# Query, key and value products of the latent vectors as three split products through the common weight ring

## The chip, the cores and the metric

The kernel runs on one core of a Trainium2 chip. The metric is the device time in microseconds (us). Of three runs before the change the median is 1682.95 us (1682.1 to 1685.35).

## The reference

An encoder of two layers works on 256 tokens of 1024 channels in float32. Each layer has three parallel branches (latent attention, a spatial gate, attention to a memory), merged by gates, and then a channel mixer: a dense SwiGLU in layer 0, eight experts with the best two per token in layer 1. The change touches the latent attention's projections:

```python
def mla_branch(c_q_raw, c_kv_raw, k_r_raw, positions, g_q, g_kv, w_uq, w_uk, w_uv):
    c_q = rmsnorm(c_q_raw, g_q)                     # 256 x 384
    q = (c_q @ w_uq).reshape(b, s, MLA_HEADS, MLA_QK)   # 384 x 768
    ...
    c_kv = rmsnorm(c_kv_raw, g_kv)                  # 256 x 256
    k_nope = (c_kv @ w_uk).reshape(b, s, MLA_HEADS, MLA_NOPE)   # 256 x 512
    v = (c_kv @ w_uv).reshape(b, s, MLA_HEADS, MLA_V)           # 256 x 512
```

## The kernel before

**Split products.** Nearly all weights reach TensorE (PE) in two parts of type fp32r: ScalarE (ACT) copies a piece from its raw float32 slot into the high part `whi` (`hi_parts`, line 1352), and VectorE (DVE) takes raw minus high into the low part `wlo` (`lo_parts`, line 1723). The activations are split in the same manner: ACT writes the high part out of PSUM with the norm's gain (`norm_hi`, line 1378), DVE the low part (`norm_lo`, line 1745). `acc3` (line 650) then makes three products per pair of tiles: high by high, high by low, low by high. The native float32 products go through `acc` (line 640) instead, which needs no split: the query, key and value projections do, and a few small ones.

**The ring.** `pieces` is one list in the order of use. SyncE (SP) loads piece after piece into raw slots; in the mixer three slots take turns (`MIX_RAW`), and slots 3 to 6 are scratch of the attention, except that the pieces `("uq", l, 0)` and `("ukv", l)` come early into slots 5 and 6. Before a load SP waits until the piece that was in the slot is used up (`wait_slot`): for a split piece that is its low part being written, for an unsplit one its last product. `("uq", l, 1)` stands unsplit in the common ring after the `qx` pieces. The split parts `whi` and `wlo` have three buffers each (`SPLIT`), so that split number m may begin when PE is done with piece m - 3.

**Who splits when.** ACT and DVE run a fixed order of instructions. Between their other work they call `hi_parts(room(name))` and `lo_parts(room(name))`. `room(name)` (line 582) counts the pieces whose earlier buffers PE has released before it makes the product `name`; all of these are split there, ahead of what follows in the program. For an unsplit predecessor in the same raw slot it also asks for that one's last product.

**The stretch of the change.** In each layer PE makes, in this order: the products of the input projection (`cq`, `ckv`, `sv`, `su`, `qx`), the transposes of the spatial weights (`wsT`, line 764), the transposes of the latent vectors (`cT`, line 681), the eight products of the spatial gate (line 778), which wait for ACT's copy of `wsT` (line 1445), the query products (lines 784 to 789), and then `mixer_steps`: memory scores of head 0 (`ms`, line 862), keys and values (`k`, `v`, lines 865 to 870), and "fill" steps of 18 split products of gate and branch weights (line 796) between the small products of the attentions. ACT has in this stretch the copy of `wsT`, the copies of the query products to `q_sb` (line 1451), the exponentials of the memory scores (line 1477) and the copies of the keys. DVE copies `qx` (line 1835), writes the latent vectors with their gain into `cT` (line 1842), mixes the spatial gate (lines 1853 to 1862), takes the maxima of the scores (line 1920), scales the probabilities (line 1928) and writes the values (line 1934). DVE's steps skip `lo_parts` at `ms` and `k` (line 1914), so that its first place for it after the query products is at step `v`. PE reads the latent vectors only when all three groups of `cT` are written (line 782).

Of the kernel before, what the change touches and what calls it, by code (L numbers as in the profile page):

```python
# [33 lines left out]
F32 = mybir.dt.float32  # L34
# [186 lines left out]
def build(nc, x, mem, positions, g_mix, w_in, g_q, g_kv, w_uq, w_uk, w_uv, g_sg, w_s, b_s, g_mem,  # L221
# [26 lines left out]
    with ExitStack() as ctx:  # L248
# [3 lines left out]
        def sem(name):  # L252
            return ctx.enter_context(nc.semaphore(name))
# [130 lines left out]
        gate_row_in = [sem(f"gate_row_in{i}") for i in range(4)]  # L384
        merged_hi = sem("merged_hi")
        pos_in = sem("pos_in")
        router_in = sem("router_in")
# [47 lines left out]
        def rows(w, c0, c1, r0=0, r1=None):  # L435

            r1 = w.shape[0] if r1 is None else r1
            return w[r0:r1, c0:c1].rearrange("(k p) c -> p k c", p=P)
# [14 lines left out]
        for l in range(DEPTH):  # L453
            wi, hk = w_in[l], D // 2

            def mixer_piece(key, *parts, **how):
                piece(key, MIX_RAW, *parts, **how)
# [7 lines left out]
            half_q = H * QK // 2  # L465
            mixer_piece(("uq", l, 0), rows(w_uq[l], 0, half_q), split=False, slot=RAW - 2)
            mixer_piece(("ukv", l), rows(w_uk[l], 0, H * NOPE), rows(w_uv[l], 0, BW), split=False, slot=RAW - 1)
            for name, c0, c1 in (("cq", 0, C_KV), ("ckv", C_KV, C_SG), ("sv", C_SG + SG, C_XQ)):
                for k in range(2):
                    mixer_piece((name, l, k), rows(wi, c0, c1, k * hk, (k + 1) * hk))  # L470
            for name, c0 in (("su", C_SG), ("qx", C_XQ)):
                for n in range(2):
                    mixer_piece((name, l, n), rows(wi, c0 + n * W, c0 + (n + 1) * W))
            mixer_piece(("uq", l, 1), rows(w_uq[l], half_q, 2 * half_q), split=False)
            for n in (1, 2, 0):
# [89 lines left out]
        def free(ins, name):  # L565
            ins.then_inc(bank_free[groups[name].bank], 1)

        def gate_row(n, half):
# [49 lines left out]
        def _(pe):  # L618
# [94 lines left out]
            for l in range(DEPTH):  # L713
# [70 lines left out]
                for n in range(2):  # L784
                    w = raw_weight(("uq", l, n))[:, 0:3 * 384].rearrange("p (k c) -> p k c", k=3)
                    for t in range(T):
                        b = claim(("q", l, t, n))
                        ins = acc(b[:, 0:384], lambda k: cT[:, k, tok(t)], lambda k: w[:, k, :], 3)
                        mark(ins, ("q", l, t, n), *([("uq", l, n)] if t else []))
                def branch(n):  # L790
# [51 lines left out]
                for step in steps:  # L842
# [22 lines left out]
                    elif kind in ("k", "v"):  # L865
                        w = raw_weight(("ukv", l)).rearrange("p (i k c) -> p i k c", i=2, k=2)[:, int(kind == "v")]
                        t = step[1]
                        b = claim(name)
                        ins = acc(b[:, :], lambda k: cT[:, 3 + k, tok(t)], lambda k: w[:, k, :], 2)
                        mark(ins, name, *([("ukv", l)] if kind == "v" and t else []))  # L870
                    elif kind in ("mpT", "apT"):
# [466 lines left out]
        def _(act):  # L1338
# [43 lines left out]
            for l in range(DEPTH):  # L1382
# [61 lines left out]
                b = full(act, ("wsT", l))  # L1444
                free(nc.scalar.activation(hn[:, 1, G * P:], b[:, :], ACT.Copy), ("wsT", l))
                act.wait_ge(lat_inv, l + 1)
                for t in range(T):
# [233 lines left out]
        def _(dve):  # L1681
# [104 lines left out]
            for l in range(DEPTH):  # L1786
# [49 lines left out]
                for n in range(3):  # L1836
                    lo_parts(room(("cT", l, n)))
                    b = full(dve, ("cT", l, n))
                    for c in range(2 if n < 2 else 1):
                        k = 2 * n + c  # L1840
                        g = c_of["q"] + l * 3 + k if k < 3 else c_of["kv"] + l * 2 + k - 3
                        ins = V.tensor_scalar(cT[:, k, :], b[:, c * SEQ:(c + 1) * SEQ], cols[:, g:g + 1], None, ALU.mult)
                    free(ins, ("cT", l, n))
# [413 lines left out]
```

## Time and profile before

| what | value |
|---|---|
| median of three runs | 1682.95 us (1682.1 to 1685.35) |
| the profiled execution's own time | 1684.01 us |
| its span | 1682.3 us |
| mean granted clock of PE | 0.996 |
| busy: PE, DVE, ACT | 98%, 76%, 62% of the span |
| the mixer of layer 0 | up to about 275 us, with the latent products at 93 to 109 us |
| the mixer of layer 1 | about 440 to 700 us, with the latent products at 526 to 542 us |
| dense layer, experts | 275 to 465 us, 717 to 1675 us |

Times in the profile count from the start of the span. The busy shares say which engine has work; what a stretch costs is read from the start times of neighbouring instructions, since the products overlap in the pipeline and the duration shown for one is longer than the step from it to the next. A native product appears as two instructions.

### The profile page before, as it was taken

What the parts mean: (1) busy time and instruction counts of PE and PEld (TensorE: products, weight loads), DVE (VectorE), ACT (ScalarE), POOL (GpSimd) and SP (SyncE); (2) the same over time, 40 slices, a digit from 0 to 9 for tenths busy, and PEclk for the clock granted to TensorE, in tenths of its full rate; (3) what the DMA queues carried; (4) which work ended last, traced back from release to release, by engine and by line L of the source; (5) the groups of instructions that cost most, each with busy time, mean ns of one, the idle gap of its engine ahead of it and who ended that gap; (6) DMA issues with size and microseconds to landing.
All of it is one profiled execution on the core that took longest, in us unless ns stands there. A gap on an engine that the chain in (4) does not pass through costs nothing.

```text
span 1682.3 us, 22649 instructions
## 1 busy us (share of the span) xinstructions
PE 1649.5 (98%) x8392; PEld 1393.5 (83%) x8392; DVE 1281.7 (76%) x1173; ACT 1047.7 (62%) x948; POOL 29.9 (2%) x57
## 2 busy tenths in 40 slices
PE   7999999999999999999999999999999999999997
PEld 6977889999988788888888888888888888888885
DVE  7556567555566656688888988888888888888997
ACT  6544545333363454477777777777777777777774
POOL 1000000000000000020000000000000000000100
PEclk9999999999999999999999999999999999999999
DMA  8633578976464346679999999999999999999994
GB/s 280 204 138 114 159 232 298 301 233 228 141 191 145 124 132 198 237 288 396 389 396 387 355 391 385 361 394 389 359 382 389 368 388 368 384 392 360 391 393 160
DMA packets 241346, 496.97 MB, mean 295 GB/s; under 512 B 8502, under 2 KB 62320, under 8 KB 241280
## 3 DMA queue, kind: packets, MB, share of 16 engines
q1 hardware_dynamic: 235280, 479.23, 79.2%
q0 software_dynamic: 2624, 8.45, 1.4%
q10 hardware_dynamic: 3376, 8.39, 1.3%
q8 instruction: 43, 0.70, 0.2%
q14 instruction: 23, 0.19, 0.0%
HBM read 476.64 MB, written 19.40 MB: 295 GB/s over the span
## 4 chain that ended last, share of the span: by engine, by line
PE 94%; DVE 3%; ACT 2%; issue 1%; DMA 0%; DVEq 0%; SPq 0%; ACTq 0%
PE bank L1076 24%; PE bank L650 21%; PE bank L1109 18%; PE bank L1080 12%; PE bank L796 10%; PE bank L640 3%; PE bank L1093 1%; PE bank L909 1%; ACT whi L1352 0%; PE bank L709 0%; PE bank L880 0%; PE bank L1121 0%; ACT pbuf L1477 0%; DVE hT_lo L1745 0%; DMA hn<-in_mem 0%
## 5 line engine op out<-in xcount | busy, mean ns | idle before, releaser
L2118 DVE TENSOR_TENSOR wlo<-raw,whi 128x2048 fp32r<-128x2048 f32 x328 | 747.9, 2288 | 108.3 <-ACT whi L1581 108.2
L1581 ACT ACTIVATE whi<-raw 128x2048 fp32r<-128x2048 f32 x328 | 627.7, 1918 | 178.4 <-PE bank L1080 94.3
L1723 DVE TENSOR_TENSOR wlo<-raw,whi 128x2048 fp32r<-128x2048 f32 (+3 forms) x113 | 249.1, 2209 | 196.5 <-ACT whi L1352 196.1
L1076 PE MATMUL bank<-whi,yT_hi 128*128 128x512 f32 x896 | 354.5, 396 | 0.3 <-DVE yT_lo L2086 0.3
L1076 PE MATMUL bank<-whi,yT_lo 128*128 128x512 f32 x896 | 349.3, 390 | 0.0
L1352 ACT ACTIVATE whi<-raw 128x2048 fp32r<-128x2048 f32 (+3 forms) x113 | 208.8, 1851 | 132.0 <-PE bank L650 92.9
L1080 PE MATMUL bank<-wlo,yT_hi 128*128 128x512 f32 x896 | 240.0, 390 | 0.0
L1080 PEld LDWEIGHTS bank<-wlo,yT_hi 128*128 128x128 f32 x896 | 168.2, 188 | 35.6
L1076 PEld LDWEIGHTS bank<-whi,yT_hi 128*128 128x128 f32 x896 | 168.3, 188 | 34.0 <-issue 0.5
L1076 PEld LDWEIGHTS bank<-whi,yT_lo 128*128 128x128 f32 x896 | 168.4, 188 | 33.5
L1109 PE MATMUL bank<-whi,yT_hi 128*128 128x512 f32 x448 | 176.2, 393 | 0.0
L1109 PE MATMUL bank<-wlo,yT_hi 128*128 128x512 f32 x448 | 174.7, 390 | 0.0
L1109 PE MATMUL bank<-whi,yT_lo 128*128 128x512 f32 x448 | 174.5, 389 | 0.0
L650 PE MATMUL bank<-hT_hi,wlo 128*128 128x256 f32 x464 | 131.3, 283 | 0.0
L650 PE MATMUL bank<-hT_lo,whi 128*128 128x256 f32 x464 | 131.3, 283 | 0.0
L650 PE MATMUL bank<-hT_hi,whi 128*128 128x256 f32 x464 | 131.3, 283 | 0.0
L1109 PEld LDWEIGHTS bank<-whi,yT_hi 128*128 128x128 f32 x448 | 84.0, 188 | 25.1 <-issue 8.5
L1109 PEld LDWEIGHTS bank<-wlo,yT_hi 128*128 128x128 f32 x448 | 84.1, 188 | 17.9
L1109 PEld LDWEIGHTS bank<-whi,yT_lo 128*128 128x128 f32 x448 | 84.2, 188 | 16.2
L650 PEld LDWEIGHTS bank<-hT_hi,whi 128*128 128x128 f32 x464 | 89.0, 192 | 0.4
L650 PEld LDWEIGHTS bank<-hT_lo,whi 128*128 128x128 f32 x464 | 89.0, 192 | 0.4
L650 PEld LDWEIGHTS bank<-hT_hi,wlo 128*128 128x128 f32 x464 | 89.0, 192 | 0.0
(280 smaller groups left out, 2002.1 us busy)
## 6 DMA issues: line engine op xcount, KB each, us to landing
raw<-in_moe_w SPq DMA_DIRECT2D x336, 1024.0 KB, 7.4
raw<-in_w_in SPq DMA_DIRECT2D x36, 1024.0 KB, 5.2
raw<-in_dense_w SPq DMA_DIRECT2D x30, 1024.0 KB, 6.5
raw<-in_w_br SPq DMA_DIRECT2D x12, 1024.0 KB, 5.0
raw<-in_w_mkv SPq DMA_DIRECT2D x8, 1024.0 KB, 7.6
raw<-in_w_out SPq DMA_DIRECT2D x8, 1024.0 KB, 5.1
rows_by_slot<-qxT SPq DMA_DIRECT2D x15, 512.0 KB, 7.1
y_by_slot<-qxT SPq DMA_DIRECT2D x9, 512.0 KB, 8.0
```

Of the source, the lines that this page charges most:

```text
L640: ins = nc.tensor.matmul(bank, lhs(k), rhs(k), start=(k == 0), stop=(k == n - 1))
L650: ins = nc.tensor.matmul(bank, lhs(a, k), rhs(b, k), start=(start and k == chunks[0] and a + b == 0), stop=(stop and k == chunks[-1] and a ...
L796: ins = nc.tensor.matmul(bank, src(a, x0), w[b_][:, w0, :], start=(start and q + i == 0), stop=(stop and last))
L909: ins = nc.tensor.matmul(b[:, t * SEQ:(t + 1) * SEQ], qT[0:QK, h, tok(t)], kT[0:QK, h, :], start=True, stop=True)
L1076: nc.tensor.matmul(b[:, :], hselT[a][:, half, tok(k)], w[:, k, :], start=(half + k + a == 0), stop=False)
L1080: ins = nc.tensor.matmul(b[:, :], hselT[0][:, half, tok(k)], w[:, k, :], start=False, stop=(half == 1 and k == 3))
L1093: ins = nc.tensor.transpose(b[:, tok(c)], g32_m[:, tok(c)], ident[:, :])
L1109: ins = nc.tensor.matmul(banks[4 + n][:, :], gated_m[a][:, b_ % 2, tok(2 * half + c)], w[p][:, c, n * HALF:(n + 1) * HALF], start=(b_ + ha ...
L1352: nc.scalar.activation(whi[:, m % SPLIT, 0:floats(n)], raw[:, pieces[n][1], 0:floats(n)], ACT.Copy).then_inc(hi_ready, 1)
L1581: nc.scalar.activation(whi[:, (E0 + n) % SPLIT, :], raw[:, n % RAW, :], ACT.Copy).then_inc(hi_ready, 1)
L1723: V.tensor_tensor(wlo[:, m % SPLIT, 0:size], raw[:, pieces[n][1], 0:size], whi[:, m % SPLIT, 0:size].bitcast(F32), ALU.subtract).then_inc( ...
L2118: V.tensor_tensor(wlo[:, s, :], raw[:, n % RAW, :], whi[:, s, :].bitcast(F32), ALU.subtract).then_inc(lo_ready, 1)
```

## The change

Both operands of the query, key and value products get high and low parts. The latent vectors' high part is written by ACT into `mT[0]` (new, after the copy of `wsT`), the low part by DVE into `mT[1]` in the place of the copy to `cT`, after a wait on the new semaphore `latent_hi`. The weights `uq` and `ukv` become split pieces that stand one behind the other after the `qx` pieces in the common ring, and the early loads into slots 5 and 6 are gone. The 12 native query products of a layer become 36 split ones, the 8 native key and value products 24.

```diff
--- before.py
+++ after.py
@@ -383,6 +383,7 @@
         row_in = sem("row_in")
         gate_row_in = [sem(f"gate_row_in{i}") for i in range(4)]
         merged_hi = sem("merged_hi")
+        latent_hi = sem("latent_hi")
         pos_in = sem("pos_in")
         router_in = sem("router_in")
         gf_in = sem("gf_in")
@@ -463,15 +464,15 @@
             turn = turn if l == 0 else 0
 
             half_q = H * QK // 2
-            mixer_piece(("uq", l, 0), rows(w_uq[l], 0, half_q), split=False, slot=RAW - 2)
-            mixer_piece(("ukv", l), rows(w_uk[l], 0, H * NOPE), rows(w_uv[l], 0, BW), split=False, slot=RAW - 1)
             for name, c0, c1 in (("cq", 0, C_KV), ("ckv", C_KV, C_SG), ("sv", C_SG + SG, C_XQ)):
                 for k in range(2):
                     mixer_piece((name, l, k), rows(wi, c0, c1, k * hk, (k + 1) * hk))
             for name, c0 in (("su", C_SG), ("qx", C_XQ)):
                 for n in range(2):
                     mixer_piece((name, l, n), rows(wi, c0 + n * W, c0 + (n + 1) * W))
-            mixer_piece(("uq", l, 1), rows(w_uq[l], half_q, 2 * half_q), split=False)
+            for n in range(2):
+                mixer_piece(("uq", l, n), rows(w_uq[l], n * half_q, (n + 1) * half_q))
+            mixer_piece(("ukv", l), rows(w_uk[l], 0, H * NOPE), rows(w_uv[l], 0, BW))
             for n in (1, 2, 0):
                 for half in range(2):
                     c0 = C_GATE + n * D + half * HALF
@@ -564,6 +565,10 @@
 
         def free(ins, name):
             ins.then_inc(bank_free[groups[name].bank], 1)
+
+        def latent_gain(l, k):
+            g = c_of["q"] + l * 3 + k if k < 3 else c_of["kv"] + l * 2 + k - 3
+            return cols[:, g:g + 1]
 
         def gate_row(n, half):
             return half if n else 2 + half
@@ -782,11 +787,12 @@
                 for n in range(3):
                     read(pe, ("cT", l, n))
                 for n in range(2):
-                    w = raw_weight(("uq", l, n))[:, 0:3 * 384].rearrange("p (k c) -> p k c", k=3)
+                    w = weight(("uq", l, n), 3)
                     for t in range(T):
                         b = claim(("q", l, t, n))
-                        ins = acc(b[:, 0:384], lambda k: cT[:, k, tok(t)], lambda k: w[:, k, :], 3)
-                        mark(ins, ("q", l, t, n), *([("uq", l, n)] if t else []))
+                        ins = acc3(b[:, 0:384], lambda a, k: mT[a][:, k, tok(t)], lambda a, k: w[a][:, k, :], range(3),
+                                   True, True)
+                        mark(ins, ("q", l, t, n), *([("piece", "uq", l, n)] if t else []))
                 def branch(n):
 
                     def products(bank, src, w, chunks, start, stop, *names):
@@ -863,11 +869,13 @@
                                                    start=True, stop=True)
                         mark(ins, name)
                     elif kind in ("k", "v"):
-                        w = raw_weight(("ukv", l)).rearrange("p (i k c) -> p i k c", i=2, k=2)[:, int(kind == "v")]
+                        w = weight(("ukv", l), 4)
+                        k0 = 2 * int(kind == "v")
                         t = step[1]
                         b = claim(name)
-                        ins = acc(b[:, :], lambda k: cT[:, 3 + k, tok(t)], lambda k: w[:, k, :], 2)
-                        mark(ins, name, *([("ukv", l)] if kind == "v" and t else []))
+                        ins = acc3(b[:, :], lambda a, k: mT[a][:, 3 + k, tok(t)], lambda a, k: w[a][:, k0 + k, :], range(2),
+                                   True, True)
+                        mark(ins, name, *([("piece", "ukv", l)] if kind == "v" and t else []))
                     elif kind in ("mpT", "apT"):
                         if kind == "mpT":
                             pe.wait_ge(prob_ready, l * XH + h + 1)
@@ -1443,6 +1451,13 @@
                 hi_parts(room(("wsT", l)))
                 b = full(act, ("wsT", l))
                 free(nc.scalar.activation(hn[:, 1, G * P:], b[:, :], ACT.Copy), ("wsT", l))
+                for n in range(3):
+                    b = full(act, ("cT", l, n))
+                    for c in range(2 if n < 2 else 1):
+                        k = 2 * n + c
+                        ins = nc.scalar.activation(mT[0][:, k, :], b[:, c * SEQ:(c + 1) * SEQ], ACT.Copy,
+                                                   scale=latent_gain(l, k))
+                    ins.then_inc(latent_hi, 1)
                 act.wait_ge(lat_inv, l + 1)
                 for t in range(T):
                     for n in range(2):
@@ -1836,10 +1851,12 @@
                 for n in range(3):
                     lo_parts(room(("cT", l, n)))
                     b = full(dve, ("cT", l, n))
+                    dve.wait_ge(latent_hi, 3 * l + n + 1)
                     for c in range(2 if n < 2 else 1):
                         k = 2 * n + c
-                        g = c_of["q"] + l * 3 + k if k < 3 else c_of["kv"] + l * 2 + k - 3
-                        ins = V.tensor_scalar(cT[:, k, :], b[:, c * SEQ:(c + 1) * SEQ], cols[:, g:g + 1], None, ALU.mult)
+                        ins = V.scalar_tensor_tensor(out=mT[1][:, k, :], in0=b[:, c * SEQ:(c + 1) * SEQ],
+                                                     scalar=latent_gain(l, k), in1=mT[0][:, k, :].bitcast(F32),
+                                                     op0=ALU.mult, op1=ALU.subtract)
                     free(ins, ("cT", l, n))
 
                 dve.wait_ge(row_in, 16 * (l + 1))
```

## Rows read from the trace of the kernel before

**Rows 1.** The page: busy time by engine, and the chain of waits by line.

```profile
PE 1649.5 (98%) x8392; PEld 1393.5 (83%) x8392; DVE 1281.7 (76%) x1173; ACT 1047.7 (62%) x948; POOL 29.9 (2%) x57
...
PE bank L1076 24%; PE bank L650 21%; PE bank L1109 18%; PE bank L1080 12%; PE bank L796 10%; PE bank L640 3%; PE bank L1093 1%; PE bank L909 1%; ACT whi L1352 0%; PE bank L709 0%; PE bank L880 0%; PE bank L1121 0%; ACT pbuf L1477 0%; DVE hT_lo L1745 0%; DMA hn<-in_mem 0%
```

**Rows 2.** Timeline of PE, layer 0, from the latent transposes on (start us, us, what).

```profile
90.64 1.25 PE L681 MATMUL bank<-ident,cqkv 128*128 128x128 f32 x10
91.73 1.95 PE L778 MATMUL bank<-hn,sgv 128*128 128x128 f32 x16
93.54 7.98 PE L640 MATMUL bank<-raw,cT 128*128 128x384 f32 x24
101.36 1.03 PE L862 MATMUL bank<-mkT,qxT 128*128 128x256 f32 x4
102.22 7.03 PE L640 MATMUL bank<-raw,cT 128*128 128x512 f32 x16
...
109.32 0.40 PE L796 MATMUL bank<-wlo,hT_hi 128*128 128x512 f32 x1
...
113.22 1.02 PE L862 MATMUL bank<-mkT,qxT 128*128 128x256 f32 x4
```

**Rows 3.** The same query product in layer 1.

```profile
526.70 7.98 PE L640 MATMUL bank<-raw,cT 128*128 128x384 f32 x24
```

**Rows 4.** Timeline of PE: first of 48 split products 384 wide, and their successor.

```profile
41.51 0.33 PE L650 MATMUL bank<-whi,hT_hi 128*128 128x384 f32 x1
...
49.86 0.29 PE L650 MATMUL bank<-whi,hT_hi 128*128 128x288 f32 x1
```

**Rows 5.** Timeline of ACT, layer 0.

```profile
38.38 3.03 ACT L1378 ACTIVATE hT_hi<-bank,cols 128x256 fp32r<-128x256 f32 x8 [2.33 <-PE bank L709]
...
90.84 0.60 ACT L1445 ACTIVATE hn<-bank 128x512 f32<-128x512 f32 x1 [4.22 <-PE bank L764]
...
108.05 1.91 ACT L1352 ACTIVATE whi<-raw 128x2048 fp32r<-128x2048 f32 x1 [2.34 <-DMA raw<-in_w_br]
```

**Rows 6.** Timeline of DVE, layer 0.

```profile
39.33 3.23 DVE L1745 SCALAR_TENSOR_TENSOR hT_lo<-bank,cols,hT_hi 128x256 fp32r<-128x256 f32 x8 [0.89 <-ACT hT_hi L1378]
...
90.40 0.69 DVE L1835 COPY qxT<-bank 128x512 f32<-128x512 f32 x1 [1.46 <-PE bank L650]
...
91.28 2.05 DVE L1842 TENSOR_SCALAR cT<-bank,cols 128x256 f32<-128x256 f32 x5 [0.18 <-PE bank L681]
...
102.42 0.69 DVE L1920 TENSOR_REDUCE rmax<-bank 128x2 f32<-128x512 f32 x1 [3.71 <-PE bank L862]
...
105.94 0.62 DVE L1928 TENSOR_SCALAR pbuf<-pbuf,rrec 128x256 f32<-128x256 f32 x2
...
109.99 2.29 DVE L1723 TENSOR_TENSOR wlo<-raw,whi 128x2048 fp32r<-128x2048 f32 x1 [3.43 <-ACT whi L1352]
...
112.20 1.40 DVE L1934 TENSOR_SCALAR raw<-bank,rin 128x512 f32<-128x512 f32 x2
...
114.28 0.69 DVE L1920 TENSOR_REDUCE rmax<-bank 128x2 f32<-128x512 f32 x1 [0.68 <-PE bank L862]
```

**Rows 7.** Waits of PE: who released it, us in total, times, longest.

```profile
PE bank L640 <- DVE hn L1895: 3.6, 2, 1.8
...
PE bank L673 <- DMA cqkv<-in_g_mem: 3.3, 1, 3.3
```

**Rows 8.** A weight load in SyncE's timeline, and one kind's time to landing.

```profile
78.86 0.37 SPq L1231 DMA_DIRECT2D raw<-in_w_in  x1
...
raw<-in_w_uv SPq DMA_DIRECT2D x2, 512.0 KB, 7.3
```

**Rows 9.** Stretches of PE: length, busy (instructions), granted clock, DMA share, GB/s.

```profile
144.00:147.00 3.00, 2.85 (x25) 1.00 0.07 5
703.00:706.00 3.00, 1.89 (x14) 1.00 1.04 397
709.00:716.00 7.00, 7.00 (x35) 0.52 0.37 120
```

## The prediction

> **What bounds the kernel.** I read the page first: PE is busy for 98% of the span, and the chain of waits stays on PE almost from end to end [rows 1]. So whatever makes PE's work shorter counts in full, as long as PE doesn't have to wait for what the shorter work needs. The chain gives line 640, where the native products are, 3% of the span. I then went to the timeline of each engine around those products. PE goes without a break from the latent transposes (90.64) through the gate products (91.73), the queries (93.54), the first scores (101.36) and the keys and values (102.22) to the gate weights [rows 2]. DVE finishes the latent vectors at 91.28 + 2.05 = 93.33, which is 0.21 before PE begins the queries [rows 2, 6]: there is no slack in that place. ACT, on the other hand, sat idle for 4.22 us before it copied the spatial weights at 90.84 [rows 5]. Layer 1 repeats the stretch with the same durations (queries at 526.70) [rows 3], so I work out layer 0 and take it twice.
>
> **What PE gains.** The native queries took 101.36 - 93.54 = 7.82 us. A split product of the same width steps by (49.86 - 41.51)/48 = 0.174 us [rows 4], and 36 of them make 6.26 us: 1.56 saved. The native keys and values ran from 102.22 to about 109.09 (the second gate product starts at 109.32, the first one a step earlier): 6.87 us. The split products 512 wide step by (113.22 - 109.32)/17 = 0.229 us [rows 2], and 24 of them make 5.50: 1.37 saved. The gain per layer is 2.93 us if nothing is late.
>
> **What comes late: the latent vectors.** The order of splitting decides. Split number m waits for piece m - 3 on PE. With the new list, uq0 waits for su1 and uq1 for qx0; both are split while PE makes the qx products, as the gate pieces were in their place before, and they are smaller (1152 against 2048 elements): nothing. But ukv has to wait for qx1 alone, so `room` puts it ahead of the copy of wsT on ACT and ahead of the latent vectors on DVE. Before, the piece in that place of the ring (the first branch weights) was held back by the unsplit uq1 in its raw slot until 108.05, where ACT waited for its load [rows 5]. That restraint is gone. The data are there: SP issued a load after the low part of qx1 at 78.86, and a value weight landed in 7.3 us [rows 8], so by about 87.
> - ACT sees the end of qx1 when DVE does, at 90.40 [rows 6]. Its split of 2048 elements takes 1.91 [rows 5] to 92.3. DVE's half of a split starts 109.99 - 108.05 = 1.94 behind ACT's, at 92.34, and its next instruction 112.20 - 109.99 = 2.21 later, at 94.55 [rows 5, 6].
> - ACT copies wsT until 92.3 + 0.60 = 92.9 [rows 5] instead of 91.44. PE waits for it and makes the gate products from about 93.0 to 94.8 (1.81 for the eight [rows 2]).
> - ACT's five high parts cost 3.03/8 = 0.38 each [rows 5], done at 94.8. DVE's five low parts cost 3.23/8 = 0.40 each [rows 6], the last behind it: 94.55 + 2.02 = 96.57. PE starts the queries some 0.18 later, at 96.75 instead of 93.54: **3.2 us late**.
>
> Then the queries end at 103.01, the scores (0.86) at 103.87, keys and values at 109.37. Against 109.09 the whole gain is used up and 0.3 more.
>
> **What comes late next: the low part of the first gate weights.** That piece now follows uq0 in the split buffers and can't be split before PE is done with uq0, at about 99.9. ACT does it between its copies of the queries. DVE has no place for it until step `v`, behind the memory softmax. Before, the maxima started 102.42 - 101.36 = 1.06 after the scores, and the scaled probabilities ended at 106.56, 4.14 after that start [rows 2, 6]. Moved along: scores 103.01, maxima 104.07, probabilities done at 108.2. The low part takes 2.29: done at 110.4, and PE, ready at 109.37, starts the gate products at about 110.5. PE is now 110.5 - 109.09 = **1.4 us behind** the kernel before.
>
> **And behind that.** DVE does the low parts of both gate pieces (2 x 2.21, to 112.6), the two values (1.40, to 114.0) and the low part of the branch weights (2.2, to 116.1) before it takes the second head's maxima, where it was at 114.28 [rows 6]: 1.85 behind. From there to about 134 DVE leads: PE waited there twice for DVE's merge of the gates in all 3.6 us, 1.8 in each layer [rows 7]. So DVE's lateness of 1.85 becomes PE's, and I find nothing later in the mixer that gives it back: PE is dense or waits for the same chain.
>
> **Moved and removed at no cost.** The early loads of uq0, uk and uv leave SP's queue ahead of the cq pieces, and go behind qx. No gain: the one transfer that PE itself waited for is that of the memory's gain in the first microseconds [rows 7]; if cq had been late, it would stand there. No loss either: each load is issued when the piece three before it has its low part, here 5 us or more ahead of its split. The loads behind the first gate pieces are issued later than before, since those pieces' low parts are (110.4 for the first); with the 7.3 us of [rows 8] the next lands by 118, when ACT comes to it after the second head's exponentials. If that cover were gone, the price would be what ACT waited at 108.05, 2.34 [rows 5]. The wait on `latent_hi` on DVE holds nothing: ACT is one part ahead throughout.
>
> **Sum.** +1.85 per layer, +3.7 for two: 1684.01 + 3.7 = 1687.7 for a profiled execution. That one stood 1.06 over the median of the runs, so against the median 1682.95 + 3.7 = **1686.7 us**. Bounds of the unknown: that I carry the steps as if every handover cost the same as before, perhaps 0.6 per layer either way: 1685.4 to 1688.0 for this case.
>
> **Rivals.**
> - **Only the first stall** (0.14). If the lateness of DVE were taken up by its waits for the exponentials and the gate weights' low part were in time, 0.3 per layer is left: 1683.5. For it: DVE has idle time of 3.71 before the maxima [rows 6]. Against: the program puts nothing there.
> - **The clock** (0.18). From 90.4 to 96.75 PE would do transposes, 1.8 us of small native products, and stand idle for about 3. PE's granted clock stayed at 1.00 through a stretch of nothing but transposes (144 to 147), but after PE had been busy for 1.89 of 3.00 us at 703 to 706 it was down to 0.52 on average from 709 to 716 [rows 9], half of 2.4 GHz. Such a drop costs about 7 x 0.5 = 3.4 where PE is dense: in one layer 1690.1, in both 1693.5.
> - **Faster** (0.06): the latent vectors are ready as early as before, since DVE would reach them before the key weights' split. The point that decides is whether `room` includes ukv before the transposes; by the code it does, and with it the stretch can't be kept. If not, PE keeps 2.93 per layer: 1677.1. The branch weights that were kept out there by their slot are all that speaks for it.
>
> The Trainium skill (TensorE: Matmul & The Clock Gate, Part 4: PE-mode transpose) says that transposes don't count as activity for the clock gate. By that rule the stretch from 90.4 to 96.75 would hold hardly any counted work, and the clock rival would be the likelier case. The trace doesn't bear it out: the transposes around 144 to 147 brought no drop [rows 9]. That the change doesn't do what it says is excluded: the new tiles are fp32r like those of line 650, which stand as one instruction per product.
>
> **Chances.** The forecast has 0.62. A measurement of this kernel can tell about 0.2%, 3.4 us, from no change; the forecast's +3.7 lies just over that line, so I give 0.36 of its 0.62 to slower and 0.26 to same. Slower: 0.36 + 0.18 = 0.54; same: 0.26 + 0.14 = 0.40; faster: 0.06. The range runs from the first rival's 1683.5 to a drop of the clock in one layer with something on top, 1691.0; outside are the faster case and a drop in both layers.
>
> **What would show it.** In the changed profile: ACT's split of 2048 elements directly after the last qx product and before the copy of wsT; the queries on PE starting about 6.1 us after the latent transposes begin (2.9 before), with a wait for DVE's low parts of about 2; queries in 6.3 and keys and values in 5.5 us; a wait of about 1.1 of the first gate product for DVE's low part; the second head's maxima 1.8 later than before; a granted clock of 1.00 at 93 to 110. The prediction is wrong if the queries start before 95, if the first gate product doesn't wait, or if the mixer gives the lateness back before it ends.

## The result and the profile after

The change made the kernel slower: a median of 1689.65 us against 1682.95, ratio 1.0037 with a 95% interval of 1.0026 to 1.0048 (about +6.2 us; the two medians lie 6.7 apart). Measured once more, beside e9 to e11 (e12 below), the ratio was 1.0051 (1.0037 to 1.0065). One run each of e1 and e10 took 2763.23 and 2051.73 us at a mean granted clock of 0.558 and 0.752, and is left out of their ratios. The profiled execution took 1691.86 us, with a span of 1690.1 and a mean granted clock of 0.993.

The page first, busy times and chain. PE's busy time fell from 1649.5 to 1648.0 us against [rows 1], and the chain stays on PE: the page alone shows no new bound.

```profile
PE 1648.0 (98%) x8432; PEld 1403.0 (83%) x8432; DVE 1290.8 (76%) x1179; ACT 1059.0 (63%) x964; POOL 30.5 (2%) x57
...
PE bank L1084 24%; PE bank L655 22%; PE bank L1117 18%; PE bank L1088 12%; PE bank L802 10%; PE bank L1101 1%; PE bank L645 1%; PE bank L917 1%; PE bank L888 1%; PE bank L714 0%; DVE wlo L1738 0%; PE bank L1129 0%; ACT pbuf L1492 0%; PE bank L868 0%; DVE hT_lo L1760 0%
```

PE's timeline in layer 0 (start us, us, what; in brackets the idle time and who ended it) answers to [rows 2].

```profile
90.24 0.60 PE L769 MATMUL bank<-ident,hn 128*128 128x128 f32 x4
90.68 1.25 PE L686 MATMUL bank<-ident,cqkv 128*128 128x128 f32 x10
93.00 2.02 PE L783 MATMUL bank<-hn,sgv 128*128 128x128 f32 x16 [1.06 <-issue]
96.91 0.41 PE L655 MATMUL bank<-whi,mT_hi 128*128 128x384 f32 x1 [1.89 <-DVE mT_lo L1857]
...
98.03 0.52 PE L655 MATMUL bank<-whi,mT_hi 128*128 128x384 f32 x1
...
104.79 1.03 PE L868 MATMUL bank<-mkT,qxT 128*128 128x256 f32 x4
...
105.89 0.40 PE L655 MATMUL bank<-wlo,mT_hi 128*128 128x512 f32 x1
...
112.34 0.47 PE L802 MATMUL bank<-whi,hT_hi 128*128 128x512 f32 x1 [1.05 <-DVE wlo L1738]
...
116.50 1.02 PE L868 MATMUL bank<-mkT,qxT 128*128 128x256 f32 x4
```

The stretch begins at 90.24, as before (90.20). The spatial gate's products wait 1.06 us, the queries start at 96.91 and not at 93.54, and of the gate weights the first product waits 1.05 us for DVE's low part. The products themselves are shorter: keys and values, counted as in the prediction from the end of the scores' 0.86 us (105.66, a step of 0.23 ahead of the second product at 105.89), run to about 111.1, 5.5 us against 6.87. The queries took 104.79 - 96.91 = 7.88 us, though, not 6.3: from 98.03 on each product takes 0.52 us and not 0.33. The windows of PE (length, busy with instructions, granted clock, DMA share, GB/s) say why.

```profile
91.00:98.00 7.00, 4.05 (x31) 1.00 0.63 198
97.90:101.30 3.40, 3.40 (x13) 0.52 0.39 150
105.00:110.00 5.00, 5.00 (x24) 1.00 0.00 0
```

The granted clock was at half, 1.2 of 2.4 GHz, for 3.4 us in the middle of the queries. The same happened in layer 1 (0.66 of full speed on average over 534 to 539). Now ACT and DVE in the same stretch, against [rows 5, 6].

```profile
90.50 1.91 ACT L1360 ACTIVATE whi<-raw 128x2048 fp32r<-128x2048 f32 x1 [4.59 <-PE bank L655]
92.32 0.58 ACT L1453 ACTIVATE hn<-bank 128x512 f32<-128x512 f32 x1
92.80 1.93 ACT L1458 ACTIVATE mT_hi<-bank,cols 128x256 fp32r<-128x256 f32 x5
```

```profile
92.45 2.29 DVE L1738 TENSOR_TENSOR wlo<-raw,whi 128x2048 fp32r<-128x2048 f32 x1 [1.31 <-ACT whi L1360]
94.66 2.04 DVE L1857 SCALAR_TENSOR_TENSOR mT_lo<-bank,cols,mT_hi 128x256 fp32r<-128x256 f32 x5
...
105.86 0.69 DVE L1937 TENSOR_REDUCE rmax<-bank 128x2 f32<-128x512 f32 x1 [3.78 <-PE bank L868]
...
109.91 4.49 DVE L1738 TENSOR_TENSOR wlo<-raw,whi 128x2048 fp32r<-128x2048 f32 x2
114.31 1.40 DVE L1951 TENSOR_SCALAR raw<-bank,rin 128x512 f32<-128x512 f32 x2
115.63 2.28 DVE L1738 TENSOR_TENSOR wlo<-raw,whi 128x2048 fp32r<-128x2048 f32 x1
117.83 0.68 DVE L1937 TENSOR_REDUCE rmax<-bank 128x2 f32<-128x512 f32 x1
```

ACT splits the 2048 elements of the key and value weights at 90.50, ahead of the copy of the spatial weights (92.32) and of the latent high parts (92.80). DVE does the low part at 92.45 and the latents' low parts at 94.66. After the first head's softmax DVE has two low parts in a row (109.91), the values (114.31) and a third low part (115.63), and comes to the second head's maxima at 117.83; PE's scores for it were there at 117.5. Last, PE's waits (who released it; us in total, times, longest).

```profile
PE bank L655 <- DVE mT_lo L1857: 3.8, 2, 1.9
PE bank L645 <- DVE hn L1912: 3.6, 2, 1.8
...
PE bank L783 <- issue: 2.1, 2, 1.1
PE bank L802 <- DVE wlo L1738: 2.1, 2, 1.1
```

The first, third and fourth are new, 3.8, 2.1 and 2.1 us over both layers. ACT waits for no weight load in this stretch: as forecast, the moved loads cost nothing. The wait for the gate merge is the same 3.6 us as in [rows 7], though PE comes to it later: DVE is later by as much.

### The profile page after: what moved, and what is told of

It is laid out like the page before. It is cut to its first block, busy times and chain, and to the rows that moved or that the text cites. A ratio compares the mean times of both kernels' runs of the same rounds, so it can differ in the third digit from the quotient of the medians.

```text
span 1690.1 us, 22754 instructions
## 1 busy us (share of the span) xinstructions
PE 1648.0 (98%) x8432; PEld 1403.0 (83%) x8432; DVE 1290.8 (76%) x1179; ACT 1059.0 (63%) x964; POOL 30.5 (2%) x57
## 4 chain that ended last, share of the span: by engine, by line
PE 93%; DVE 3%; ACT 2%; issue 1%; DMA 0%; DVEq 0%; SPq 0%; ACTq 0%
PE bank L1084 24%; PE bank L655 22%; PE bank L1117 18%; PE bank L1088 12%; PE bank L802 10%; PE bank L1101 1%; PE bank L645 1%; PE bank L917 1%; PE bank L888 1%; PE bank L714 0%; DVE wlo L1738 0%; PE bank L1129 0%; ACT pbuf L1492 0%; PE bank L868 0%; DVE hT_lo L1760 0%
## 5 line engine op out<-in xcount | busy, mean ns | idle before, releaser
L1738 DVE TENSOR_TENSOR wlo<-raw,whi 128x2048 fp32r<-128x2048 f32 (+3 forms) x119 | 259.0, 2182 | 190.9 <-ACT whi L1360 190.5
L1360 ACT ACTIVATE whi<-raw 128x2048 fp32r<-128x2048 f32 (+3 forms) x119 | 217.3, 1829 | 143.8 <-PE bank L655 107.9
```

The lines of the kernel that those rows point to most:

```text
L1360: nc.scalar.activation(whi[:, m % SPLIT, 0:floats(n)], raw[:, pieces[n][1], 0:floats(n)], ACT.Copy).then_inc(hi_ready, 1)
L1738: V.tensor_tensor(wlo[:, m % SPLIT, 0:size], raw[:, pieces[n][1], 0:size], whi[:, m % SPLIT, 0:size].bitcast(F32), ALU.subtract).then_inc( ...
```

## The experiments

The table reads the timelines of layer 0 in each kernel, in us after its first transpose of the spatial weights (whose start lies between 88.3 and 90.2 from run to run, with the arrival of the first data). "Third product" is PE's third product of memory probabilities and values, the one that waits for DVE's gate merge; "between" is the time from DVE's second maxima to it. e1 to e4, e5 to e8 and e9 to e12 were each timed on one chip, beside the kernel before, so kernels of different groups are compared by their ratios.

| kernel | queries start | DVE's second maxima | third product | between | ratio to before (95%) |
|---|---|---|---|---|---|
| before | 3.34 | 24.08 | 43.81 | 19.73 | 1 |
| changed | 6.67 | 27.59, fall | 47.33 | 19.74 | 1.0037 (1.0026 to 1.0048) |
| e1 | 4.34 | 23.69 | 43.44 | 19.75 | 1.0005 (0.9996 to 1.0015) |
| e2 | 6.67 | 26.73, fall | 46.46 | 19.73 | 1.0025 (1.0015 to 1.0036) |
| e3 | 6.67 | 26.03 | 45.77 | 19.74 | 1.0036 (1.0023 to 1.0049) |
| e4 | 4.34 | 24.68 | 44.41 | 19.73 | 1.0017 (1.0009 to 1.0026) |
| e5 | 4.34 | 23.47 | 43.86 | 20.39 | 1.0014 (1.0004 to 1.0025) |
| e6 | 4.34 | 23.47 | 44.01 | 20.54 | 1.0021 (1.0013 to 1.0030) |
| e7 | 4.34 | 23.58 | 43.68 | 20.10 | 1.0003 (0.9994 to 1.0012) |
| e8 | 4.34 | 23.57 | 43.46 | 19.89 | 1.0010 (1.0001 to 1.0019) |
| e9 | 4.34 | 22.60 | 42.34 | 19.74 | 0.9989 (0.9980 to 0.9999) |
| e10 | 3.84 | 22.47 | 42.21 | 19.74 | 1.0007 (0.9998 to 1.0017) |
| e11 | 3.84 | 23.07 | 42.94 | 19.87 | 1.0005 (0.9995 to 1.0015) |
| e12, the changed kernel again | 6.67 | 27.60, fall | 47.33 | 19.73 | 1.0051 (1.0037 to 1.0065) |

"Fall" marks a fall of the clock within the queries of that profile, 1.56 us of lateness (7.88 - 6.32, the latter from e1, where the scores start at 10.66). e3 has the changed kernel's order without one: 45.77, 1.96 behind before. Layer 1 gives the same picture to within 0.2 us, except where the text says otherwise.

The 19.7 us of "between" are not DVE's work alone. DVE's timeline of e1 (transposes at 88.37) has waits for ACT in them, 1.09 us for the exponentials of each of three heads and 1.47 us for one split:

```profile
112.06 0.69 DVE L1936 TENSOR_REDUCE rmax<-bank 128x2 f32<-128x512 f32 x1
...
114.05 0.17 DVE L1942 RECIPROCAL rrec<-rsum 128x2 f32<-128x2 f32 x1 [1.09 <-ACT pbuf L1492]
...
116.34 2.29 DVE L1738 TENSOR_TENSOR wlo<-raw,whi 128x2048 fp32r<-128x2048 f32 x1 [1.47 <-ACT whi L1360]
...
121.13 0.17 DVE L1942 RECIPROCAL rrec<-rsum 128x2 f32<-128x2 f32 x1 [1.09 <-ACT pbuf L1492]
```

So where texts below speak of DVE's queue or chain behind the second maxima, it is a chain through DVE and ACT.

**The order of the splits.** ACT's and DVE's splits of ukv are put behind the latent vectors.

```diff
-                hi_parts(room(("wsT", l)))
                 b = full(act, ("wsT", l))
...
                     ins.then_inc(latent_hi, 1)
+                hi_parts(room(("wsT", l)))
                 act.wait_ge(lat_inv, l + 1)
...
                 for n in range(3):
-                    lo_parts(room(("cT", l, n)))
                     b = full(dve, ("cT", l, n))
...
                 for t in range(T):
-                    lo_parts(room(("sg", l, t)))
                     b = full(dve, ("sg", l, t))
...
+                lo_parts(room(("sg", l, 1)))
                 for t in range(T):
                     read(dve, ("sg", l, t))
```

> The changed kernel, but the key and value weights' split stands behind the latent vectors on ACT and behind the spatial gate's first step on DVE. Theory of the order (the split of ukv ahead of the latents costs PE about 3.2 us per layer): the queries start 3.7 to 4.3 us after the latent transposes instead of 6.2, the granted clock stays at 1.00 in both mixers, and since the gate weights' low part is still behind the first softmax, PE keeps a wait of about 1 us there: ratio to the kernel before 0.9985 to 1.0000 (some 1680.5 to 1683). Rival, the split products or the two-engine latents cost what was lost in themselves, wherever the weights are split: 1.002 or more, and the queries still start 5 us or more after the latent transposes.

PE's timeline of e1 (its transposes start at 88.37):

```profile
92.71 0.41 PE L655 MATMUL bank<-whi,mT_hi 128*128 128x384 f32 x1 [0.86 <-DVE mT_lo L1856]
...
106.58 0.47 PE L802 MATMUL bank<-whi,hT_hi 128*128 128x512 f32 x1 [1.06 <-DVE wlo L1738]
...
131.81 1.10 PE L645 MATMUL bank<-pbuf,mv 128*128 128x256 f32 x4 [1.81 <-DVE hn L1911]
```

The queries start 4.34 after the transposes of the spatial weights, which is 3.90 after those of the latents and in the range of the theory (3.7 to 4.3, counted from the latter), and the latents cost PE 0.86 instead of 1.89. The wait for the gate weights is still 1.06. The third product is 0.37 ahead of before and no longer 1.96 behind, and no fall of the clock lies in the queries. The ratio, 1.0005, is no change against before; of the 0.9985 to 1.0000 expected its interval only touches the upper end. By the timeline this one order makes up the whole loss outside the clock, 2.33 us of the third product per layer, since what it moves also brings DVE's second maxima forward. That the split products cost the loss in themselves is refuted.

**The gate weights' low part.** One line ahead of DVE's mixer steps.

```diff
+                lo_parts(room(("q", l, 1, 1)))
                 for step in steps:
```

> The changed kernel, but DVE makes the low part of the first gate weights ahead of the first memory scores instead of at the value step. Theory that DVE's queue behind that place makes the second half of the loss: the wait of about 1.05 us of the first gate product goes away, the second head's maxima come some 2 us earlier, and it is 1.2 to 1.8 us per layer faster than the changed kernel (ratio to before about 1.0015 to 1.0025 with the clock still falling). Rival, the wait is hidden in what DVE delays later anyway: the total stays within 0.5 us of the changed kernel, ratio 1.0035.

The gate weights' wait is gone from PE's list. The clock fell in layer 0's queries as in the changed kernel, and DVE's second maxima came 0.86 earlier than there, not 2, and the third product 0.87 earlier (46.46 against 47.33), less than the 1.2 to 1.8 expected. Layer 1, where e2's clock did not fall in the queries, agrees: 44.89 against 45.80 in e3. The ratio, 1.0025, is at the edge of the theory's. Both orders changed at once (e1 and e2 together):

> Both orders mended: the latents ahead of the ukv split, and the gate weights' low part ahead of the first scores. Theory of the order: PE is 1 us late at the queries and gains 2.9 by their end, 1.5 to 2 us per layer ahead of the kernel before, which DVE's chain up to the gate merges lets through only in part: ratio 0.9975 to 0.999. Rival, DVE's chain from the second head on sets the time whatever comes before it: ratio 0.9995 to 1.0005, with longer waits of PE for the gate merge.

DVE's timeline of e4 (transposes at 90.12) shows why its third product came 0.97 later than e1's.

```profile
101.75 2.29 DVE L1738 TENSOR_TENSOR wlo<-raw,whi 128x2048 fp32r<-128x2048 f32 x1
103.95 0.68 DVE L1937 TENSOR_REDUCE rmax<-bank 128x2 f32<-128x512 f32 x1
...
107.26 0.17 DVE L1943 RECIPROCAL rrec<-rsum 128x2 f32<-128x2 f32 x1 [2.42 <-ACT pbuf L1492]
...
114.80 0.68 DVE L1937 TENSOR_REDUCE rmax<-bank 128x2 f32<-128x512 f32 x1
```

The low part at 101.75 stands where PE's scores were ready at about 101.9: it pushes the maxima to 103.95, all of the first softmax with them, and the second maxima to 24.68. A low part moved out of one wait had gone into another. After that PE waited four times for DVE's probabilities, 4.6 us in all, and the clock fell behind those waits in both layers. Both expectations missed, the theory's 0.9975 to 0.999 and the rival's 0.9995 to 1.0005: the ratio was 1.0017 (1.0009 to 1.0026).

**What DVE does behind the second maxima.** e5 takes the branch weights' low part behind the second softmax, e6 also gives the values' copies to ACT (first and last line below).

```diff
+                        free(nc.scalar.activation(v_sb[:, t, :], b[:, :], ACT.Copy, scale=rin[:, 2 + t:3 + t]), name)
...
-                    if kind not in ("O", "ms", "as", "k"):
+                    if kind not in ("O", "ms", "as", "k") and step != ("fill", 0):
                         lo_parts(room(name))
...
-                        free(V.tensor_scalar(v_sb[:, t, :], b[:, :], rin[:, 2 + t:3 + t], None, ALU.mult), name)
```

> The kernel of e1_latents_first, but DVE makes the low part of the first branch weights after the second head's softmax instead of ahead of its maxima. Theory that from the second head on the time up to the gate merges is set by DVE's queue: the second head's maxima come 1 to 2 us earlier, DVE's wait of 1.47 us for ACT's next split goes, and the wait of PE for the merge ends 1 to 1.5 us earlier in each layer: 2 to 3 us faster than e1, ratio to before 0.9985 to 0.9990 if the clock holds. Rival, the end of that stretch is set by ACT's splits and exponentials: PE's third memory product starts at the same 43.4 us after the transposes as in e1, ratio 1.0005.

> The kernel of e5 with the two copies of the values on ACT in the place of DVE (1.40 us of DVE's queue in each layer, ACT idle for 4.85 us behind that place). Theory of DVE's queue: another 1.0 to 1.4 us per layer at PE's third memory product, ratio 0.9970 to 0.9980. Rival, once the branch weights are out of the way DVE has slack ahead of the second head, and the move brings under 0.3 us per layer.

DVE's timeline of e5 (transposes at 89.70), the second maxima and the merge that frees PE's third product:

```profile
113.17 0.69 DVE L1936 TENSOR_REDUCE rmax<-bank 128x2 f32<-128x512 f32 x1 [1.89 <-PE bank L868]
...
132.73 1.40 DVE L1911 SCALAR_TENSOR_TENSOR hn<-cT,bank 128x512 f32<-128x512 f32 x2
```

Both theories missed; e6's rival, that the move brings under 0.3 us, is what came. The maxima come at 23.47 in e5 and e6 alike, since now DVE waits there for PE's scores (1.89 and 3.21 us), and the low part that was pushed behind them lengthens the way to the third product to 20.4 and 20.5 us: 1.47 of its 2.2 us fill DVE's wait for ACT's split there, the rest comes on top. DVE's work was moved from a stretch in which it could wait into one in which it mostly can't. In both kernels the clock fell in each layer after the third product.

**One part alone.** e7 keeps keys and values native, their weights unsplit; e8 adds the moves of e5 and e6.

> One part of the change alone, with the order of e1: the queries in split products, keys and values native as in the kernel before, their weights unsplit in slot 6. Against e1, PE loses the 1.37 us of keys and values, DVE loses one low part of 2.2 us from its queue. Theory of DVE's queue: what PE gives back there costs nothing, since it would wait for DVE anyhow; the third memory product starts 0.5 to 2 us earlier than in e1 in each layer, ratio to before 0.9980 to 0.9995. Rival, PE's work counts in full: 1.4 us per layer slower than e1, ratio 1.0020.

> Queries alone (e7) with the branch weights' low part later and the values' copies on ACT (e6). Theory of DVE's queue: its work ahead of the third memory product is the least of all kernels here, so that PE's own work sets the time: 1.5 to 2.5 us per layer faster than before at the end of the mixer, ratio 0.9970 to 0.9985. Rival, it equals e6, since both are then bound by PE, with e6 the faster by the 1.37 us of keys and values per layer.

e7's third product stands at 43.68 in layer 0 and 43.33 in layer 1, against 43.44 and 43.45 in e1, though PE has lost 1.37 us of shorter keys and values again: 0.2 later in one layer, 0.1 earlier in the other. The rival's 1.4 us per layer is refuted; PE's gain on keys and values brought nothing that shows. The gain of 0.5 to 2 us that I expected didn't come either, since DVE waited 1.97 us for PE's second scores. e8 was no faster than before (1.0010); it stands level with e7 and far from the 0.9970 to 0.9985 expected. Its rival missed too: its third product came 0.55 ahead of e6's, not 1.37 behind.

**The low part into an idle time.** From the table follows what to aim at: DVE's second maxima earlier, with nothing moved behind them. In e9 the gate weights' low part goes into DVE's wait for the first exponentials.

```diff
                                         ALU.mult).then_inc(max_ready, 1)
+                        if step == ("ms", 0):
+                            lo_parts(room(("q", l, 1, 1)))
                         if kind == "ms":
```

> The kernel of e1, with DVE's low part of the first gate weights put into its wait of 2.43 us for the first exponentials (behind the first maxima, ahead of the scaling). In e4 the same work stood ahead of the maxima and pushed them back by 2 us. Theory (what counts is when DVE begins the second head's maxima; from there its own work to PE's third memory product is 19.7 us in e1 and can't shrink): the wait of 1.05 goes, the second scores of PE come at 21.4 instead of 22.4 us after the transposes, the third memory product at 42.2 to 42.5 instead of 43.4: 1 us per layer faster than e1, ratio to before 0.9985 to 0.9995 if the clock holds. Rival: DVE's queue is full anyhow, what is put in here comes out behind, and the product starts at 43.4 as in e1, e5 and e6: ratio 1.0005.

DVE's timeline of e9 (transposes at 90.09):

```profile
101.84 0.69 DVE L1936 TENSOR_REDUCE rmax<-bank 128x2 f32<-128x512 f32 x1
...
102.64 2.28 DVE L1738 TENSOR_TENSOR wlo<-raw,whi 128x2048 fp32r<-128x2048 f32 x1
105.16 0.17 DVE L1944 RECIPROCAL rrec<-rsum 128x2 f32<-128x2 f32 x1 [0.23 <-ACT pbuf L1492]
...
112.69 0.68 DVE L1936 TENSOR_REDUCE rmax<-bank 128x2 f32<-128x512 f32 x1
```

The low part (102.64) fills the wait, of which 0.23 is left, and the first maxima stay where PE's scores put them. The second maxima come at 22.60 and the third product at 42.34, both as the theory had it. The ratio is 0.9989 (0.9980 to 0.9999): faster than the changed kernel; against before the gain is so small that the interval ends at 0.9999. The fastest single run took 1676.68 us. The profiled one had the clock fall behind the third product, in both layers; its windows of PE around that product in layer 0:

```profile
128.00:132.00 4.00, 1.99 (x10) 1.00 0.84 313
132.00:135.50 3.50, 3.07 (x7) 0.52 0.02 5
```

The first of these windows ends 0.43 us ahead of the third product (132.43); the last section compares windows that end with it.

> e9, and the queries wait for the first two groups of latent low parts alone, the keys for the third. Theory: the queries start 0.4 us earlier (3.9 instead of 4.3 after the transposes), and of that up to 0.4 reach the third memory product: ratio 0.9980 to 0.9995. Rival: DVE's full queue swallows it, the product stays where e9 has it.

> e10 with the values' copies on ACT. With DVE's queue full ahead of the second maxima, 1.4 us less of it there should now count, which it did not in e6, where PE's second scores were the later: third memory product 0.3 to 1 us earlier than in e10. Rival: PE's second scores stay the later, no change against e10. For the clock: e5 and e6 had their third waits of PE lengthened and lost 1.7 us in each layer to a fall of the clock behind them; if PE's wait before the third memory product grows here, so will that loss.

In e10 the queries start 0.50 earlier, and 0.13 of that reaches the third product: the rival is nearer. The ratio is 1.0007. Its runs lay between 1682.2 and 1684.8, and none reached e9's fast ones; the only loss that its profile shows is the clock behind the third product, as in e9's, so why its runs are slower than e9's is not shown. In e11 the copies of the values on ACT delay ACT's split of the branch weights, DVE waits 1.82 us for it, and the second maxima come at 23.07: the move costs 0.73 us at the third product in layer 0 and 0.58 in layer 1, in place of bringing 0.3 to 1. PE's wait before that product grew with it; behind it the clock fell for twice as long in layer 0 (132 to 139) and not at all in layer 1.

**The clock.** Products that do no work in PE's two gaps, nothing else changed.

```diff
+                keep_clock(("sg", l, 0), 4)
                 pe.wait_ge(vn_ready, T * (l + 1))
...
+                keep_clock(("q", l, 0, 0), 8)
                 for n in range(3):
                     read(pe, ("cT", l, n))
```

> The changed kernel with native 128-wide products that do no work put into the two gaps of PE, 4 ahead of the spatial gate's and 8 ahead of the queries. They leave the order as it is. Theory that the rest of the loss, and its spread over the runs, is the granted clock falling to half for 3.4 us per layer: no stretch below 1.00 at 93 to 110 us, every run near 1686.7, ratio 1.0022. Rival, the spread has another cause and the clock falls all the same: ratio 1.0037 and runs from 1686.6 to 1692.3 as before.

PE's windows of e3:

```profile
91.00:98.00 7.00, 6.79 (x49) 1.00 0.70 200
97.90:101.30 3.40, 3.40 (x21) 1.00 0.16 60
569.00:574.00 5.00, 4.76 (x14) 0.66 0.12 14
```

No fall in the queries of either layer. The window of 91 to 98 starts 2.65 us after e3's transposes, but 0.76 after the changed kernel's; placed alike (89.11 to 96.11), PE was busy for 6.72 of 7.00 us against 4.05. But the clock fell in layer 1 after the third product (0.66 of full speed on average over 569 to 574). The runs reached from 1685.4 to 1691.4, ratio 1.0036: the expected 1.0022 was missed. That is hardly under the changed kernel's 1.0037 and 1.0051, and the intervals overlap, so that the sum of what the falls in the queries cost is not settled by the times; their place and their 1.56 us are read from the profiles.

> The changed kernel once more, beside e9 to e11 on the same chip. Ratio 1.0026 to 1.0048 as in the first measurement, single runs between 1686.6 and 1692.3 in steps of about 1.7 us, one step for each fall of the clock to half for 3.4 us in the query products; a profile with no such fall would show the third memory product 45.7 us after the transposes, 1.9 behind the kernel before.

The ratio was 1.0051, above the 1.0026 to 1.0048 expected though its interval reaches down to 1.0037, and the five runs lay between 1688.6 and 1692.2, higher than expected at the low end. The profile has a fall in layer 0's queries, and two more behind the third products of both layers, which the first profile had not. In layer 1, with none in the queries, the third product stands at 45.79: 1.89 behind the 43.90 of that layer before. PE did the same there as in layer 0, where the clock fell: it was busy for 4.04 of the 7.00 us from 527.3 to 534.3, and the clock stayed at 1.00 then and from 534 to 541, through the queries. Of the six stretches of this kind in the profiles of the changed kernel, e2 and e12, four were followed by a fall and two, in layer 1 of e2 and of e12, were not. That e3's two had none is therefore in line with its added products, but would be weak evidence alone. The other side is firmer: in the 18 stretches of e1 and e4 to e11, with PE busy for 6.1 to 6.6 of the 7 us, there was no fall in the queries.

## Why the prediction was right, and where its size was off

**The gain and the first stall: right.** Each product was as short as forecast. The queries were forecast at 96.75 and started at 96.91; PE's wait for the latents' low parts is 1.89. e1 shows the cause: with ukv's split behind the latents 2.3 us of the 3.3 are gone.

**The second stall: right in place and size.** A wait of 1.05 was measured against "about 1.1", and in the kernel without a fall of the clock in the queries (e3) the second scores start 24.74 after the transposes, 1.7 behind before, against 1.4 forecast.

**DVE behind it: right, and the table makes it a rule of this kernel.** I took DVE to be 1.85 us late at the second maxima and to lead from there. It was 1.95 late in e3, and the kernels that left DVE's work behind the maxima alone came to the third product 19.7 us later in both layers, e7 and e11 in layer 1 alone (20.10 and 19.87 in layer 0). "DVE leads" has to be read as the chain through DVE and ACT, with 4.7 us of DVE's waits for ACT in it. The forecast of +1.85 per layer was +1.96, +1.90 and +1.89 in the three places without a fall (both layers of e3, layer 1 of e12).

**The clock: the term that was mis-sized.** I held the fall against the forecast as a rival, with a chance of 0.18, and priced one at 3.4 us per layer from the stretch of 7 us in [rows 9]. It took place beside the forecast, not in its stead, in both layers of the first profile, so that the forecast's sign of a granted clock of 1.00 at 93 to 110 failed. Its price was half of what I took: 3.4 us at half clock, 1.56 us on the queries. With two of them, 3.7 + 3.1 = 6.8, against 1691.86 - 1684.01 = 7.85 measured between the two profiled executions. At the third product PE is 3.52 us behind in layer 0 and 3.46 in layer 1, 6.98 in all, which the order (1.96 and 1.89) and two falls (3.1) explain. The remaining 0.9 lies outside this stretch; 0.5 of it comes behind the experts' last products, and no run explains it. The +6.2 to +6.7 of the seven runs is the order's 3.85 and, as an estimate, between one and two falls more. It was luck that the sum with one drop, 1690.1, came so near to the measured 1689.65: the price was taken twice too high and the number of falls too low. What I underrated is in my own numbers: PE idle for some 3 us of 6.5 with only transposes and small native products in between (4.05 busy of 7.00 us, measured), against 1.89 of 3.00 ahead of the fall in [rows 9]. Such a stretch makes a fall likely and not certain, as layer 1 of e2 and e12 shows. The sentence of the Trainium skill on transposes (TensorE: Matmul & The Clock Gate, Part 4: PE-mode transpose), which I set aside by the stretch at 144 to 147 alone (it says that they don't count as busy in the same way, less than I made of it), would have given the clock the better chance; the trace after agrees with it in so far as this stretch of transposes and waits was followed by a fall, and doesn't show that transposes were the reason.

**The rivals.** "Only the first stall" is refuted by the 1.05 us wait. "Faster" is refuted by ACT's split at 90.50, which stands where `room` was said to put it.

## What to carry to other kernels

Where a planner places work by "as soon as its buffers are free", a change that frees the buffers earlier also moves that work, here a 2.2 us low part ahead of the latents that PE was waiting for. Before making the bound engine's work shorter, look for the next place where it waits for another engine: if the chain up to there has no slack, the gain ends in the wait, and only what is put into the other engine's idle times (as in e9) moves without cost. Each new wait of PE should be priced with the slower clock that can follow it.

## What the runs showed of the hardware

I had not expected the clock to fall so often behind waits of some 2 us. Behind the third memory product it fell in both layers of e4, e5, e6, e9, e10 and e12 and in one layer of e3, e8 and e11, 15 of 28 places; in the profiles of the kernel before, the changed kernel, e1, e2 and e7 it didn't. PE's windows of the kernel before at that place:

```profile
130.00:134.00 4.00, 2.02 (x11) 1.00 0.82 307
134.00:137.50 3.50, 3.49 (x16) 1.00 0.02 5
```

This first window ends with the third product (134.01), that of e9 above (1.99 of 4.00 us) does not, and so the two must not be set side by side. With windows of 4 us that end with the product:

| kernel and layer | window | PE busy | clock behind it |
|---|---|---|---|
| before, 0 | 130.01 to 134.01 | 2.01 | full |
| e8, 1 | 560.38 to 564.38 | 2.01 | fell |
| e9, 0 | 128.43 to 132.43 | 1.56 | fell |
| e2, 0 | 130.80 to 134.80 | 1.33 | full |
| e4, 0 | 130.53 to 134.53 | 0.66 | fell |
| e11, 1 | 563.91 to 567.91 | 0.66 | full |

How busy PE was just ahead of the product does not separate the falls from the rest: at 2.01 and at 0.66 us there is one of each. Single runs of one kernel lie up to 7.8 us apart (e9's, 1676.68 to 1684.43), and a PE that comes earlier to the same wait did not always gain: e10, 0.13 us ahead of e9 by the timelines in each layer, was slower by its runs. What decides in one execution whether the clock falls is open; no run here separates it.
